# Where the causal mask of the stick-breaking attention is added: VectorE after the scores, or TensorE inside the accumulation

## The reference, cut to what matters

```python
z = einsum('bhtd,bhsd->bhts', qb, kb) * scale            # scale = 1/8
causal = s_idx[None, :] < t_idx[:, None]
log_1mb = where(causal, log_sigmoid(-z), 0.0)
suffix = cumsum(log_1mb, axis=3, reverse=True) - log_1mb
log_a = where(causal, log_sigmoid(z) + suffix, -inf)
out = einsum('bhts,bhsd->bhtd', exp(log_a), vb)
```

## Time and profile before

| what | value |
|---|---|
| median of three executions | 2049.36 us |
| the profiled execution | 2047.99 us |
| its span | 2046.3 us |
| TensorE busy | 1990.0 us, 97% of the span |
| VectorE busy | 1141.6 us, 56% |
| ScalarE busy | 813.1 us, 40% |
| mean granted TensorE clock | 0.992 of full speed |
| attention stage, first score to last product | 1061.3 to 1265.5 us |

### The profile page before, as it was taken

The page is one execution under the profiler, slowest core; times in us unless marked ns, Lnnn a source line. Parts: engine busy times, 40 slices in busy tenths (PEclk is TensorE's granted clock), DMA queues, the critical chain, the costliest instruction groups (busy, mean ns, idle before and its releaser), DMA issues.

```text
span 2046.3 us, 25997 instructions
## 1 busy us (share of the span) xinstructions
PE 1990.0 (97%) x10510; PEld 1612.1 (79%) x10510; DVE 1141.6 (56%) x1841; ACT 813.1 (40%) x1369; POOL 109.3 (5%) x131
## 2 busy tenths in 40 slices
PE   8999999999999999999999999999999999999997
PEld 6777767788888888888877777787889788888886
DVE  5567766644455444422648888884555465444323
ACT  5244431533344222322437777453444453222321
POOL 0000000000010000000200001330120020000000
PEclk9999999999999999999999999999999999999998
DMA  7111112233323333332222221112234223333331
GB/s 283 47 40 44 52 52 62 74 96 93 99 72 103 93 93 94 94 95 84 91 80 63 62 62 52 52 42 72 73 115 123 72 83 93 93 93 93 93 95 60
DMA packets 49431, 170.55 MB, mean 83 GB/s; under 512 B 5520, under 2 KB 8080, under 8 KB 48928
## 3 DMA queue, kind: packets, MB, share of 16 engines
q1 hardware_dynamic: 48816, 166.73, 27.3%
q0 software_dynamic: 496, 2.16, 0.3%
HBM read 166.77 MB, written 2.10 MB: 83 GB/s over the span
## 4 chain that ended last, share of the span: by engine, by line
PE 89%; DVE 8%; issue 1%; ACT 1%; DMA 0%; SPq 0%; DVEq 0%
PE acc L1780 58%; PE bank L1780 17%; PE bank L1869 2%; PE bank L1942 1%; DVE w_lo L1066 1%; PE bank L2081 1%; PE bank L2018 1%; DVE bank L1144 1%; PE bank L2116 1%; PE bank L1915 1%; PE bank L2274 1%; PE bank L2309 1%; PE bank L1802 1%; DVE residual L1150 1%; PE bank L1945 1%
## 5 line engine op out<-in xcount | busy, mean ns | idle before, releaser
L1066 DVE TENSOR_TENSOR w_lo<-w_raw,w_hi 128x1024 fp32r<-128x1024 f32 (+2 forms) x306 | 364.7, 1195 | 300.2 <-ACT w_hi L591 299.7
L1780 PE MATMUL acc<-act_hi,w_hi 128*128 128x512 f32 (+1 forms) x1160 | 457.1, 394 | 16.9 <-DVE w_lo L1066 9.1
L1780 PE MATMUL acc<-act_hi,w_lo 128*128 128x512 f32 (+1 forms) x1160 | 445.0, 384 | 0.0
L1780 PE MATMUL acc<-act_lo,w_hi 128*128 128x512 f32 (+1 forms) x1160 | 444.7, 383 | 0.0
L591 ACT ACTIVATE w_hi<-w_raw 128x1024 fp32r<-128x1024 f32 (+2 forms) x306 | 314.7, 1030 | 204.9 <-PE acc L1780 179.7
L1780 PEld LDWEIGHTS acc<-act_hi,w_hi 128*128 128x128 f32 x1160 | 218.7, 188 | 71.4 <-issue 15.7
L1780 PEld LDWEIGHTS acc<-act_hi,w_lo 128*128 128x128 f32 x1160 | 218.4, 188 | 46.8
L1780 PEld LDWEIGHTS acc<-act_lo,w_hi 128*128 128x128 f32 x1160 | 218.9, 189 | 45.8 <-issue 2.2
L1780 PE MATMUL bank<-act_hi,w_hi 128*128 128x512 f32 (+1 forms) x520 | 192.8, 371 | 1.2 <-DVE w_lo L1066 1.2
L1780 PE MATMUL bank<-act_lo,w_hi 128*128 128x512 f32 (+1 forms) x520 | 190.9, 367 | 0.0
L1780 PE MATMUL bank<-act_hi,w_lo 128*128 128x512 f32 (+1 forms) x520 | 190.9, 367 | 0.0
(11 more groups left out here) (447 smaller groups left out, 3034.2 us busy)
## 6 DMA issues: line engine op xcount, KB each, us to landing
w_raw<-w_all SPq DMA_DIRECT2D x282, 512.0 KB, 3.5
w_raw<-w_all SPq DMA_DIRECT2D x16, 384.0 KB, 3.2
residual<-xT SPq DMA_DIRECT2D x8, 256.0 KB, 7.0
cmp_w_k<-w1k SPq DMA_DIRECT2D x1, 2048.0 KB, 8.4
cmp_w_v<-w1v SPq DMA_DIRECT2D x1, 2048.0 KB, 12.6
w_raw<-w_all SPq DMA_DIRECT2D x8, 256.0 KB, 2.7
out_t<-residual SPq DMA_DIRECT2D x16, 128.0 KB, 1.7
ret_decay<-decay POOLq DMA_DIRECT2D x4, 256.0 KB, 3.4
```

The source lines that it names most:

```text
L1066: TT(WL[:, c % RAW_RING, 0:nb * P], WR[:, c % RAW_RING, 0:nb * P], WH[:, c % HI_RING, 0:nb * P].bitcast(F32), ALU.subtract).then_inc(s_lo, 1)
L1780: ins = MM(bank[:, cols], w[:, at, k * P:(k + 1) * P], x, start=first and r == 0 and k == 0, stop=last and r == 2 and k == nb - 1)
```

## The change

Lines that begin with - are of the kernel before.

```diff
-SB_ORDER = [("abs", b) for b in range(4)] + [("exp", b) for b in range(4)] + [("abs", 4), ("exp", 4)]
-SB_ORDER += [("log", b) for b in range(5)]
...
+        IDS = place("sb_ident_r", [P, P], 102, F32R)
+        SBM = place("sb_mask_r", [P, P], 102.5, F32R)
...
 # ScalarE, stage sb_qkv, slot 3
+                    A(IDS[:], ident, ACT.Copy)
+                    A(SBM[:], const("sb_mask"), ACT.Copy).then_inc(sem("sb_masks"), 1)
...
 # ScalarE, chain_to_log(p, slots)
-                for what, b in SB_ORDER:
-                    if (what, b) == ("log", 0) and p:
-                        act.wait_ge(sem("sb_pv"), p)
-                        A(OSB[:, p - 1, :], PS[5][:], ACT.Copy).then_inc(sem("sb_out"), 1)
-                    {"abs": sb_abs, "exp": sb_neg_exp, "log": sb_log}[what](p, b)
+                for b in range(5):
+                    sb_abs(p, b)
+                for b in range(5):
+                    sb_neg_exp(p, b)
+                if p:
+                    act.wait_ge(sem("sb_pv"), p)
+                    A(OSB[:, p - 1, :], PS[5][:], ACT.Copy).then_inc(sem("sb_out"), 1)
+                if slots > 1:
+                    split_hi(nxt)
+                    nxt += 1
+                for b in range(5):
+                    sb_log(p, b)
                 if p:
                     out_square(p - 1)
-                for _ in range(slots - 1):
+                if slots > 2:
                     split_hi(nxt)
                     nxt += 1
...
 # VectorE
-            def sb_hide(p):
-                for b in range(5):
-                    dve.wait_ge(sem("sb_log"), sb_step(p, "abs", b))
-                    TT(diagonals(b), diagonals(b), hidden_keys(b), ALU.add).then_inc(sem("sb_hidden"), 1)
...
-            def chain_to_scan(p, freed):
+            def chain_to_scan(p):
                 for b in range(5):
                     sb_log_beta(p, b)
                     if b:
                         sb_scan(p, b - 1)
-                    if b == 1:
-                        leaves(freed)
                 sb_scan(p, 4)
...
-                sb_hide(p)
-                chain_to_scan(p, turn[0])
+                leaves(turn[0])
+                chain_to_scan(p)
...
 # TensorE: the scores now leave the accumulation open (stop=False), and
+            def masked(b):
+                for _, i, at in parts_of(b):
+                    ins = MM(PS[b][:, at + i * P:at + (i + 1) * P], IDS[:], SBM[:], start=False, stop=True,
+                             skip_group_check=True)
+                ins.then_inc(sem("sb_scored"), 1)
 
             def long_blocks(p):
                 for b in range(2):
-                    scored(b, parts_of(b), p).then_inc(sem("sb_scored"), 1)
+                    scored(b, parts_of(b), p)
+                for b in range(2):
+                    masked(b)
...
 # middle_blocks: scores of banks 2 and 3, then masked(2), masked(3)
 # last_block(p, False): second half of bank 4, then masked(4)
...
+            pe.wait_ge(sem("sb_masks"), 1)
             long_blocks(0)
```

More of the change, by code:

```diff
@@ L111 @@
 SB_RING = 4
-SB_ORDER = [("abs", b) for b in range(4)] + [("exp", b) for b in range(4)] + [("abs", 4), ("exp", 4)]
-SB_ORDER += [("log", b) for b in range(5)]
-def sb_step(p, what, b):
-    return p * len(SB_ORDER) + SB_ORDER.index((what, b)) + 1
 MIXER = {1: ["a0", "a1"], 2: ["a2", "a3"], 3: ["a4", "a5"], 4: ["a6", "a7"], 6: ["s0", "s1"], 7: ["s2", "s3"],
@@ L395, in parts_of @@
                     [(0, 1, 0), (1, 1, 2 * P)])[b]
[L397 to L403, removed]
         def row_exp(n):
@@ L873, in sb_neg_exp @@
             def sb_neg_exp(p, b):
-                act.wait_ge(sem("sb_log"), sb_step(p, "abs", b))
+                act.wait_ge(sem("sb_log"), p * 15 + b + 1)
                 A(sb_tmp(b), sb_tmp(b), ACT.Exp, scale=-1.0).then_inc(sem("sb_log"), 1)
             def sb_log(p, b):
-                act.wait_ge(sem("sb_log"), sb_step(p, "exp", b))
+                act.wait_ge(sem("sb_log"), p * 15 + b + 6)
                 A(sb_tmp(b), sb_tmp(b), ACT.Ln, bias=1.0).then_inc(sem("sb_log"), 1)
@@ L1535, in sb_log_beta @@
             def sb_log_beta(p, b):
-                dve.wait_ge(sem("sb_hidden"), p * 5 + b + 1)
-                dve.wait_ge(sem("sb_log"), sb_step(p, "log", b))
+                dve.wait_ge(sem("sb_log"), p * 15 + b + 11)
                 STT(out=sb_tmp(b), in0=PS[b][:], scalar=0.0, in1=sb_tmp(b), op0=ALU.min, op1=ALU.subtract).then_inc(
                     sem("sb_log_beta"), 1)
-            def sb_hide(p):
-                for b in range(5):
-                    dve.wait_ge(sem("sb_log"), sb_step(p, "abs", b))
-                    TT(diagonals(b), diagonals(b), hidden_keys(b), ALU.add).then_inc(sem("sb_hidden"), 1)
             def sb_scan(p, b):
@@ L2081, in scored @@
                     ins = MM(PS[b][:, at:at + (i + 1) * P], qkv("q", p)[rows, i * P:(i + 1) * P], qkv("k", p)[rows, 0:(i + 1) * P],
-                             start=at == 0, stop=True, skip_group_check=True)
+                             start=at == 0, stop=False, skip_group_check=True)
                 return ins
+            def masked(b):
[3 more added lines that the diff above has]
+                ins.then_inc(sem("sb_scored"), 1)
             def long_blocks(p):
                 for b in range(2):
-                    scored(b, parts_of(b), p).then_inc(sem("sb_scored"), 1)
+                    scored(b, parts_of(b), p)
+                for b in range(2):
+                    masked(b)
             def middle_blocks(p):
@@ L2091, in middle_blocks @@
                     for b in (2, 3):
-                        ins = scored(b, parts_of(b)[j:j + 1], p)
-                        if j:
-                            ins.then_inc(sem("sb_scored"), 1)
+                        scored(b, parts_of(b)[j:j + 1], p)
+                for b in (2, 3):
+                    masked(b)
             def last_block(p, first):
@@ L2101, in last_block @@
                     pe.wait_ge(sem("sb_first_half"), p + 1)
-                    scored(4, parts_of(4)[1:2], p).then_inc(sem("sb_scored"), 1)
+                    scored(4, parts_of(4)[1:2], p)
+                    masked(4)
             def turned(p, b):
```

## The result

The changed kernel takes 2061.66 us (median of 5 runs, 2058.45 to 2063.21), the kernel before in the same comparison 2049.88 us (5 runs, 2047.99 to 2052.76). The ratio is 1.0055, 95% interval 1.0044 to 1.0066: slower by 9.0 to 13.5 us. I had said 2058.5 us, 9.7 us slower. Of the 3.2 us between 2058.5 and the median, 1.1 belong to the kernel before, which I had put at 2048.8.

A forecast was written before the change was run, and what follows sets the result against it. TensorE, busy in 97% of the span, was taken to bound the kernel. 8.3 us of masks plus 1.4 us of last-turn waiting gave 9.7 us, forecast 2058.5 us; own range 2056 to 2062, 8 in 10 range 2054 to 2064.

The forecast's parts named there:

- That VectorE's additions are worth nothing in seven of eight pairs: Five VectorE additions per pair, 1.39 us, 11 us over 8 pairs: off the path in seven, since TensorE does not wait there.
- 64 masks paid in full on TensorE, 8.3 us: 64 fp32r mask matmuls on TensorE: 1.02 us in each of seven turns plus 1.2 for pair 0, together 8.3 us.
- The saving at the weight tile: Third mask group ahead of a weight tile: the tile's first matmul gets 0.10 us cheaper, leaving 0.18 of 0.28.
- The moved rounding waits for the tile and holds the logs: Turn 6, ScalarE: rounding waits some 1.5 us for TensorE's first tile, logs queued behind it; last turn adds 1.4 us of waiting.
- 0.6 us to spare in a full turn: Full turn: TensorE needs bank 4 at T + 28.4, ready at T + 27.8, so the delay is hidden; first turn 0.2 to spare.
- rival (b): Steady turns start to wait, about 0.9 us in each of seven: 16 us slower, 2065 us; chance 0.12.
- The clock and the hole: Waits ahead of pair 7's transposes grow from 2.7 to about 5 us; lower clock costs up to 3 us more, 2061.5.
- Rival (a): TensorE masks at 0.08 us each, 5.1 us, plus the last turn's 1.4: 6.5 us slower, 2055 us; chance 0.14.
- Rival (c): Not slower: masks vanish in TensorE's shape-change pauses, leaving 3 us; last pair gains 2.1. Then +1 us, 2050.5; chance 0.06.

The follow-up runs named there:

- the run without masks: Kernel before with VectorE's five mask additions per pair left out and put nowhere; ratio 0.9995 (0.9986 to 1.0004) to the kernel before.
- the run with one group: Masks on TensorE, ScalarE and VectorE in the old order, all eight masks of a pair behind its last score; ratio 1.0034 to the kernel before.
- The run with the late rounding: Changed kernel with both slot roundings behind the logs again; ratio 1.0041 (1.0028 to 1.0054) to the kernel before.
- the run with the order alone: Kernel before, masks still on VectorE, with only the changed kernel's orders of ScalarE and VectorE; ratio 1.0007 (0.9998 to 1.0016) to the kernel before.
- the doubled masks: Changed kernel with each mask matmul run twice with half the mask, 64 matmuls more; ratio 1.0082 (1.0068 to 1.0096) to the kernel before.
- pair 7 alone: Kernel before with only pair 7's masks on TensorE and VectorE's additions left out for that pair; ratio 0.9997 (0.9988 to 1.0006) to the kernel before.
- f32 masks: Changed kernel with its masks as f32 matmuls straight from the constants, two passes each; ratio 1.0099 (1.0085 to 1.0112) to the kernel before.
- masks with the old order: Masks on TensorE as in the changed kernel, ScalarE and VectorE in the order of the kernel before; ratio 1.0028 (1.0017 to 1.0039) to it.

## Why the prediction was right

**That VectorE's additions are worth nothing in seven of eight pairs**: right, shown by the run without masks, whose turns are 25.63 us to the hundredth.

**64 masks paid in full on TensorE, 8.3 us**: right in kind, low in size. Measured 1.59 + 7 x 1.17 = 9.8 us. Per turn I had 1.02: I priced the first two groups by the pair of masks that another fp32r mask followed (0.28 in the earlier trace rows), where the pair followed by f32 work (0.37) was the right row; that weights\*v behind them changes the shape too is the reading of the run with one group. That is 0.09 too little for each of two groups. The saving at the weight tile was 0.06, not 0.10, and the price of one mask more 0.11, not 0.14. Group by group it is 0.37, 0.59 and 0.22 where I had 0.28, 0.56 and 0.18. For pair 0 I had 1.2 and 1.6 came: ahead of the loop scores follow scores, and each group breaks into a run that had no change of shape at all.

**The moved rounding waits for the tile and holds the logs**: right. log_beta at T + 18.3 worked out, T + 18.55 measured; bank 4 at T + 27.8 worked out, T + 28.06 measured; 1.4 us added beyond the masks, 2.64 - 1.17 = 1.5 measured. The run with the late rounding shows that this one move is the cause of these 2.45 us at log_beta, and the run with the order alone shows it without masks.

**0.6 us to spare in a full turn**: right for the transposes and incomplete. Between the last exp and the next scores stand ScalarE's two copies of transposed banks, 1.07 us, which I left out. They made TensorE wait 0.24 us in turn 0, where I had counted 0.2 to spare. In turn 6 the last exp ends at 1246.35, 0.55 us ahead of its transposes at 1246.90, as I had it, but the copies end at 1247.33, only 0.1 us ahead of the scores. So waits in every turn, rival (b), were 0.1 us away and not 0.6.

**The clock and the hole**: I had up to 3 us more as an end, and waits of about 5 us. My own terms give 2.7 + 1.4 = 4.1, and 3.7 came. In the changed kernel the clock fell one bank earlier than before (a stretch, columns as in the earlier trace rows, and TensorE's timeline):

```profile
1272.00:1273.00 1.00, 0.94 (x4) 0.69 (x4) 1.00 (x3) 0.47 (x2) 0.00 (x0) 0.56 0.00 0
```

```profile
1272.06 1.09 PE L1854 MATMUL bank<-const_cols,evacuated 128*128 128x128 f32 x4 [1.10 <-ACT evacuated L872]
1273.22 1.12 PE L1854 MATMUL bank<-const_cols,tmp_a 128*128 128x128 f32 x4
```

Bank 3's transposes took 1.16 us from start to start and so filled the 0.5 us that TensorE had waited for bank 4's exp. The stretch from bank 4 to the end of the products then took 3.98 us against 4.52: 0.5 us gained there by chance, and given back in the wait for row_rstd. That a lower clock in this place can cost 3 us is not borne out: between 3.31 and 4.97 us for the stretch, at most 0.4 us are left at row_rstd.

**The sum**: 9.8 (masks) + 1.5 (last pair) + 0.3 (turn 0) - 0.5 (clock) = 11.1, the 11.0 of the stage; up to row_rstd it is 11.6, and the ratio gives 9.0 to 13.5. My 9.7 lies in the lower part of that. The step that was mis-sized is the masks' price, by 1.5 us. Rival (a), 0.08 us a mask, is out by the doubled masks. Rival (c) is half right for pair 7 alone: with the old order its masks do fall into the hole and bank 4 comes 1.4 us earlier, but in the other pairs there is no hole, and groups between two other shapes cost 0.15 us each on top instead of vanishing in the change.

## What to carry to other kernels

Ask of each move which engine has the hole, pair by pair: the same 1.4 us of VectorE work was free seven times and on the path once, and the same 1.2 us of TensorE work was paid seven times and, with the old order, free once. Price a small matmul with its neighbours, 0.11 us for one more of the kind and 0.15 to 0.19 us for opening a group among other shapes, and take the row whose follower is like yours. And when an instruction that waits for another engine is moved ahead of a chain in a strict order, add its releaser's time to the chain: the slot rounding cost 1.06 us in either place, but ahead of the logs it waited 2 us more, and the last pair came 2.45 us later. And measure a stage up to the next step that another engine sets: 2.6 us won at the end of this one were 1.5 us there.

## What the runs showed of the hardware that was not expected

f32 masks cost the same 0.11 us per pass of 128 columns as fp32r masks per matmul, and their groups cost more to open (0.19 against 0.15 us), although the neighbours of the two groups shown are f32; being alike in type bought nothing.

The stretch from bank 4's transposes to the end of the products varied by 1.7 us between profiles of kernels with the same work in it, by whether and when the granted clock fell from 1.00 to 0.50, the 1.2 GHz level. It took 3.3 us in the three profiles in which the clock stayed at 1.00, 4.97 in three in which it fell during the products, and 3.98 to 4.93 in the four in which it fell earlier. It fell in profiles with 2.7 us of waits ahead (before), with 3.1 to 4.2 (changed, new order alone, f32 masks, one group), with 2.1 (late rounding) and with only 1.6 (no masks), and did not fall in the two with 0.7 us (masks with the old order, pair 7 alone); but with the masks doubled it did not fall either, behind waits of 4.2 us. These runs do not settle what decides it, so a gain or loss of 1.7 us there is not to be put down to an edit, and here all but 0.4 us of it vanished in the wait for row_rstd.
